# Building both halves of a rotation table on POOL instead of one half on DVE

## The reference, cut to what matters

```python
def s5_mixer(u, lam_re, lam_im, log_dt, b_re, b_im, c_re, c_im, d_skip, w_glu, b_glu):
    uf = u.reshape(bsz, L, N_SSM_GROUPS, SSM_GROUP)            # 64 groups of 16 channels
    lam_bar = jnp.exp(lam * dt)                                # one complex factor for each of 64 x 64 states
    b_bar = ((lam_bar - 1.0) / lam)[..., None] * b
    bu = jnp.einsum('blgc,gpc->blgp', uf, b_bar)
    _, h = lax.associative_scan(combine, (a, bu), axis=1)      # h[t] = lam_bar * h[t-1] + bu[t]
    y = jnp.real(jnp.einsum('blgp,gcp->blgc', h, c))
    ...
```

## Time and profile before

| | us |
|---|---|
| median of 3 runs | 3728.03 (3727.52 to 3743.22) |
| the profiled execution, its own time | 3726.59 |
| its span | 3724.8 |
| PE busy | 3596.1 (97%) |
| DVE busy | 2437.0 (65%) |
| ACT busy | 1728.0 (46%) |
| POOL busy | 278.1 (7%) |

### The profile page before, as it was taken

One profiled execution on the slowest core, in us unless ns is written; L12 is line 12 of the kernel. 1 busy time (PEld: TensorE's weight loads), 2 busy tenths in 40 slices (PEclk: granted clock), 3 DMA queues, 4 the chain that ended last, 5 costly groups with the idle time before them and its releaser, 6 DMA issues. The chain is left out here.

```text
span 3724.8 us, 56085 instructions
## 1 busy us (share of the span) xinstructions
PE 3596.1 (97%) x23128; PEld 3255.6 (87%) x23128; DVE 2437.0 (65%) x3618; ACT 1728.0 (46%) x2283; POOL 278.1 (7%) x316
## 2 busy tenths in 40 slices
PE   6988999999999999999999999999999999999998
PEld 6977889899998988998888888889899888888887
DVE  8765666566566665566766767765556577576676
ACT  4334444344444444445544535543544555454453
POOL 6640000000000220001000000022000100000000
PEclk9988999999999999999999999999999999999999
DMA  4221445555555453343555555544434355555554
GB/s 175 91 81 46 156 177 180 189 186 180 191 184 184 152 193 137 138 163 129 187 189 192 190 192 187 188 158 176 163 144 139 140 184 186 186 187 184 189 180 151
DMA packets 90942, 616.44 MB, mean 165 GB/s; under 512 B 10048, under 2 KB 12864, under 8 KB 33344
## 3 DMA queue, kind: packets, MB, share of 16 engines
q1 hardware_dynamic: 90688, 612.85, 46.2%
HBM read 610.72 MB, written 2.10 MB: 165 GB/s over the span
## 5 line engine op out<-in xcount | busy, mean ns | idle before, releaser
L2343 DVE TENSOR_TENSOR wlo<-raw,whi 128x2048 fp32r<-128x2048 f32 (+3 forms) x421 | 922.8, 2192 | 297.9 <-ACT whi L2163 291.7
L1879 PE MATMUL gemm<-x_pair,whi 128*128 128x512 f32 x2816 | 997.8, 398 | 8.8 <-DVE x_pair L2506 5.1
L2163 ACT CAST whi<-raw 128x2048 fp32r<-128x2048 f32 (+3 forms) x422 | 767.1, 1820 | 270.6 <-DMA raw<-in_stream_dram 267.1
L1880 PE MATMUL gemm<-x_pair,wlo 128*128 128x256 f32 x2816 | 791.6, 281 | 0.0
L1879 PEld LDWEIGHTS gemm<-x_pair,whi 128*128 128x128 f32 x2816 | 530.2, 188 | 133.9 <-issue 5.5
L1880 PEld LDWEIGHTS gemm<-x_pair,wlo 128*128 128x128 f32 x2816 | 534.2, 190 | 0.8
L1879 PE MATMUL gemm<-f_pair,whi 128*128 128x512 f32 x1408 | 494.3, 396 | 0.0
L1880 PE MATMUL gemm<-f_pair,wlo 128*128 128x256 f32 x1408 | 395.0, 281 | 0.0
L1565 DVE TENSOR_TENSOR wlo<-raw,whi 128x2048 fp32r<-128x2048 f32 (+2 forms) x149 | 330.2, 2216 | 85.2 <-ACT whi L1499 84.9
L1499 ACT CAST whi<-raw 128x2048 fp32r<-128x2048 f32 (+2 forms) x150 | 276.1, 1842 | 99.4 <-DMA raw<-in_stream_dram 99.4
L1879 PEld LDWEIGHTS gemm<-f_pair,whi 128*128 128x128 f32 x1408 | 264.1, 188 | 63.1 <-DVE wlo L2343 0.2
(11 more groups left out here) (526 smaller groups left out, 7154.2 us busy)
## 6 DMA issues: line engine op xcount, KB each, us to landing
raw<-in_stream_dram SPq DMA_DIRECT2D x446, 1024.0 KB, 4.8
raw<-in_stream_dram SPq DMA_DIRECT2D x96, 896.0 KB, 4.5
raw<-in_stream_dram SPq DMA_DIRECT2D x32, 768.0 KB, 4.2
raw<-in_stream_dram SPq DMA_DIRECT2D x16, 960.0 KB, 4.6
raw<-in_stream_dram SPq DMA_DIRECT2D x4, 952.0 KB, 4.7
xT<-in_hT_dram SPq DMA_DIRECT2D x4, 544.0 KB, 10.2
xT<-in_hT_dram SPq DMA_DIRECT2D x1, 2176.0 KB, 9.3
out_dram<-xT SPq DMA_DIRECT2D x3, 512.0 KB, 2.9
```

The source lines that it names most:

```text
L1879: pe.matmul(both, whi[:, slot(n), k * P:k * P + P], pairs[:, :, c, :], start=(k == 0), stop=False, skip_group_check=True)
L1880: return pe.matmul(bank(use)[:, 0:T2], wlo[:, slot(n), k * P:k * P + P], pairs[:, 0, c, :], start=False, stop=(k == nk - 1), skip_group_ch ...
L2163: act.copy(whi[:, slot(n), 0:wide], raw[:, slot(n), 0:wide]).then_inc(w_hi, 1)
L2343: dve.tensor_tensor(wlo[:, slot(n), 0:wide], raw[:, slot(n), 0:wide], whi[:, slot(n), 0:wide].bitcast(F32), ALU.subtract).then_inc(w_lo, 1)
```

## The change

The late half's eight steps go from DVE to POOL. POOL runs steps 0 to 5 behind `back(0)`, `decay_of(1)` and `c_powers(1)`, and steps 6 and 7 behind `back(1)`, `decay_of(2)` and `c_powers(2)`. Two waits are new, for the memory that is shared: ACT waits for the whole late half ahead of its first square, in stage 9, and DVE ahead of scaling the result of stage 11.

```diff
-LATE_AT = {1: (0, 3), 2: (3, 4), 3: (4, 6), 5: (6, 7), 7: (7, 8)}
+LATE_AT = {0: (0, 6), 1: (6, 8)}
...
                     if c < 7:
                         decay_of(c + 1)
                         c_powers(c + 1)
+                    if c in LATE_AT:
+                        rotations(pool, 1, tmp_late, late_part, late_to, LATE_SPANS, *LATE_AT[c])
...
                         if i >= 3:
                             act.wait_ge(l_added, i - 2)
+                        if i == 1:
+                            act.wait_ge(late_to, len(LATE_SPANS) + 1)
                         act.activation(sql[:, min(i, 2) - 1, :], lat[:, i, :], ACT.Square).then_inc(l_squared, 1)
...
                     dst = u1[:, n, :] if n < 8 else lat[:, n - 8, :]
+                    if n == 11:
+                        dve.wait_ge(late_to, len(LATE_SPANS) + 1)
                     dve.tensor_tensor(dst, bank(USE0["in", n])[:, 0:T1], rstd0[:, :], ALU.mult).then_inc(bank_free, 1)
...
                     else:
                         side(n)
-                    if n in LATE_AT:
-                        rotations(dve, 1, tmp_late, late_part, late_to, LATE_SPANS, *LATE_AT[n])
```

## The result

The changed kernel takes 3743.86 us (median of 20 runs, 3718.88 to 3752.84), the kernel before 3728.93 (20 runs, 3712.56 to 3743.22). The ratio is 1.0031, with a 95% interval of 1.0017 to 1.0045: 6 to 17 us slower, 11.6 in the middle. That is inside the 0.5% that I called no change, and outside the range of 3717 to 3741. The profiled execution took 3734.23 us, its span is 3732.4 against 3724.8.

What follows compares the result with a forecast made beforehand. PE, busy 97% of the span, was taken to bound the kernel. 22.9 us of small waits on DVE would come back as one wait on POOL, costing 0.2 us net from 3728.03: forecast 3728, range 3717 to 3741.

Steps and rivals of the forecast that it cites:

- DVE's removal: Stages 4 to 9: without the late half on DVE, PE's waits on DVE go, worth 22.9 us.
- the sum of 22.9 us: Stages 4 to 9: PE's excess waits on DVE, 2.0 + 10.7 + 4.6 + 5.6 us, all counted as gain.
- ACT's wait in stage 9 as what decides: Stage 9: ACT waits for POOL's late half, holding `feed(2)` and stage 10; PE stands still about 20 us.
- POOL's entry into the loop: Ahead of `back(0)`: POOL's earlier work unchanged, `c_powers(0)` ends at 73.55 and POOL goes on without waiting for DVE.
- 1.1 for `lo(8)`: Start of `back(0)`: 1.1 us added because DVE's `lo(8)` should overlap it.
- POOL's work from there, 52.6 us: POOL's loop from `back(0)` to the late half's end: 52.6 us with stalls, late half ready at 127.3.
- The clock behind the wait, 2.5 us: Around stage 10: granted clock falls after PE's new wait, costing 2.5 us, so stage 10 starts in effect at 132.4.
- the 0.2 of my sum: Stage 10's start: in effect 132.4 where it was 132.21, so the change costs 0.2 us.
- Behind stage 10 nothing differs. So the shift at stage 10 is the shift at the end.: After stage 10: stages keep their length, so the 0.2 us shift carries to the end.
- Hiding whole (3705): Late half fits in POOL's pauses, whole 22.9 us gained, 3705; chance 0.06, partial gains over 18.6 us included.
- the clock being kept low for the whole pair behind the wait: Behind the 20 us wait the whole pair runs at 0.77, 2.5 us more, 3731; chance 0.2 inside the forecast's.
- rival 2: POOL enters its loop at 83.93 as before because `states(0)` does not move forward; stage 10 at 149.5, 3745; chance 0.08.

Runs made afterwards that it cites:

- after_again: The changed kernel unchanged, traced once more; not timed, tile 20 at 299.31 us in its trace.
- no_late_half: The changed kernel with POOL writing zeros into the late half, its rotation steps left out; ratio 0.9948 against the kernel before, -19.4 us.
- no_act_wait: The changed kernel with the squares of stages 9 to 13 in other memory, so ACT does not wait; ratio 0.9974 against the kernel before.
- steps_later: The changed kernel with three late-half steps behind `back(0)` and five behind `back(1)`; ratio 1.0039 against the kernel before, +14.5 us.
- waits_only: The kernel before with the two new waits of ACT and DVE, DVE still building the late half; ratio 0.9998 against the kernel before.
- all_behind_back0: The changed kernel with all eight late-half steps behind `back(0)`; ratio 0.9998 against the kernel before, -0.7 us.
- pe_kept_busy: The changed kernel with 53 unread matrix products filling PE's waits in stage 9; ratio 1.0010 against the kernel before, +3.7 us.
- shared: The changed kernel with squares and late scratch tile moved, DVE building steps 0, 1, 7 and POOL 2 to 6; ratio 0.9961 against the kernel before.
- shared_thinner: As shared, with only steps 4 and 5 behind `back(1)`, step 6 on DVE, step 7 on POOL behind `back(2)`; ratio 0.9964 against the kernel before.
- before_plus_5: The kernel before with 5 unread matrix products ahead of `feed(2)` in stage 9; not timed, tile 20 at 295.74 us in its trace.

## Why the prediction was wrong, step by step

- *DVE's removal.* Right up to stage 6. Stage 4 started at 48.55 (I had 48.7), stage 6 at 67.34 (67.2), stage 8 at 88.12 (88.3). That stage 8 fits is luck of this trace: in after_again and the seven other kernels built on after it starts at 89.8 to 92.5, because PE waits for `back(0)`. So the sum of 22.9 us is 4 too high as a gain to be had; no_late_half gave 19.
- *ACT's wait in stage 9 as what decides.* Right for this order of POOL's work, and shown: no_act_wait without it (stage 10 comes 11.4 us sooner), steps_later with the other wait gone (nothing gained), waits_only with the wait and without its cause. But PE did not stand still once for some 20 us with ACT behind it. It stopped twice, 10.97 us for `back(1)` and 9.94 us for ACT, and all_behind_back0 shows that the first becomes the limit when ACT's wait ends 10.5 us sooner: both hang on POOL's queue.
- *POOL's entry into the loop, "it goes on at 73.55", with 1.1 for `lo(8)`.* Mis-sized: 78.28 instead of 74.65. I had taken it that POOL's work ahead of the loop does not change. It did: DVE without its rotation steps runs three subtractions in a row, and each shuts POOL out (3.6 us). `c_powers(0)` takes 1.1 us longer, as much as I had added for `lo(8)`. The Trainium skill, "SBUF — State Buffer", section "Who interferes with whom", has a DVE instruction with two SBUF inputs contend with a GpSimd instruction that reads SBUF, under an exclusive lock. The trace agrees, with 2.67 us three times where `lo` takes 2.32 to 2.35 and POOL's own instruction 0.62. I had used this rule for the moved steps only.
- *POOL's work from there, 52.6 us.* 51.8 measured, 78.28 to 130.07. The stalls I counted came: three of about 2 us.
- *The clock behind the wait, 2.5 us.* A little small: 3.2 from the feed's start to that of stage 11 (15.14 us for 11.94), of which 1.8 are in the feed. With 0.7 more here, and the late half 2.8 us later, stage 12 is 3.6 us late, against the 0.2 of my sum.
- *"Behind stage 10 nothing differs. So the shift at stage 10 is the shift at the end."* This step failed. In after, after_again, steps_later and pe_kept_busy, from tile 12 to tile 18 takes 2.8 to 5.0 us longer than before (3.8 in after, of which 1.1 up to tile 13 are still the clock behind the wait in stage 9), and from tile 18 to tile 20 1.5 to 1.8 us longer. It is granted clock, in places where the work is unchanged. With the 3.6 us at stage 12 the 4.0 us behind it make the 7.6 of the trace; the three others have 8.7 to 9.8 against the first trace of before. The runs have 11.6, with an interval from 6.3 to 16.8.
- *The range.* Its upper end, 3741, was the bound of POOL's sum with 2 us for the runs. The trace of after lies in it; the median over the runs does not. The granted clock of stages 15 and 16 and of the end of the phase was no term of mine, and 2 us is small for runs that spread over 30.
- *The rivals.* Hiding whole (3705) fell, as did the clock being kept low for the whole pair behind the wait: 0.93, not 0.77. The slower end (rival 2) had the right sign and a wrong mechanism: `states(0)` did move forward, to 72.5.

What stays open is why the granted clock drops longer in stages 15 and 16 of some kernels. It isn't chance (after and after_again agree), not PE's stop in stage 9 (pe_kept_busy), not the waits (waits_only), and a shift of 4 or 5 us at tile 12 by itself did not bring it. Nor does it need a late stage 10: shared and shared_thinner start stage 10 more than 20 us earlier than before and have it too, with 19.0 and 19.8 us from tile 17 to tile 18 where before has 16.6 and after 19.1. One mark goes with it in all fourteen traces. No trace in which PE stands idle for 3.4 to 3.6 us ahead of that stretch has the excess. The eight in which it stands for 4.6 to 4.9 us all have some, but from 0.3 us (before_plus_5) and 0.8 (all_behind_back0) to 3.2 (shared_thinner). So the longer stop goes with the drop but does not settle its length, and which one leads to the other was not tested. The drop between 250 and 290 us has no such mark: no_act_wait, free of the first, has 1.8 us of it.

## What to carry to other kernels

An engine's idle time is not a place for work until the work has a deadline: here the moved steps fitted POOL's free time over the phase, and not the 33 us until a memory reuse wanted the table. Before a move, look at who shares memory with what is now produced later; giving the squares another place turned 7.6 us lost into 6.4 gained at tile 20, with the same engines at work. And when DVE is relieved, recompute what its neighbour POOL can still do: subtractions that come back to back shut POOL out as the steps did that were taken away.

## What the runs showed of the hardware

- The same instructions of PE took 322.5 or 328.7 us, in two executions of the same kernel (after, after_again), both at a granted clock of 1.00. The record of the granted clock doesn't show this. The 128x512 products in waits_only, which has the longer stretch, have 399 ns each, and 391 before.
- Behind a long stop of PE the granted clock stood at one half, and the feed took 3.69 us for 1.90. Filling the stop with unread products kept it at 1.00: 11.95 us from the feed to stage 11, where the kernel with the stop has 15.14 and the one before 11.94.
- Under three two-input subtractions of DVE in a row (2.3 us each), POOL got one instruction of 0.62 us done for each.
